# Output projections of a decoder trunk: the last two units run token chunk by token chunk, with three fill buffers, a root on ScalarE and feature-major input and output

## The reference, cut to what matters

```python
def rms_norm(x, gain):
    return x * lax.rsqrt(jnp.mean(x * x, axis=-1, keepdims=True) + 1e-6) * gain
for i in range(4):
    hp, hs = rms_norm(xp, norm_g[i]), rms_norm(xs, norm_g[i])
    # mixer i % 3: q, k, v, g = split(h @ w_in); o = mixer(q, k, v)
    xp = xp + (op * silu(g)) @ w_out      # op: 2048, 1024, 1536, 2048 columns
    xs = xs + ...
```

## Time and profile before

| | |
|---|---|
| median of 3 runs | 3680.8 us (3678.0 to 3686.5) |
| the profiled execution | 3687.3 us |
| its span | 3685.5 us |
| mean granted PE clock | 0.945 |
| PE busy | 3283.7 us, 89% |
| POOL busy | 749.5 us, 20% |

### The profile page before, as it was taken

How to read it: one execution, slowest core, us unless ns; L and a number is a source line. 1 busy time by engine, 2 the same in 40 slices (tenths; PEclk the granted TensorE clock), 3 DMA queues, 4 the chain that set the end, 5 groups by cost and what they waited for, 6 DMA issues and landing times.

```text
span 3685.5 us, 56759 instructions
## 1 busy us (share of the span) xinstructions
PE 3283.7 (89%) x20193; PEld 2945.7 (80%) x20193; DVE 1456.4 (40%) x3286; ACT 1192.5 (32%) x2294; POOL 749.5 (20%) x476
## 2 busy tenths in 40 slices
PE   4999999997996999999968799969799999999788
PEld 3979798886996777777747688859697979798688
DVE  4161514235234334344434566642515161514431
ACT  4232313223123444444432344531323232323211
POOL 3101111113333111110003322233311202011341
PEclk7999999997998999999987899979899999999799
DMA  3647465557212444444443012131124242424611
GB/s 110 226 141 253 141 229 164 198 183 236 90 43 71 128 130 131 130 133 136 136 134 119 18 57 73 56 105 39 39 87 142 86 139 86 129 91 129 226 60 68
DMA packets 512941, 450.90 MB, mean 122 GB/s; under 512 B 24598, under 2 KB 460598, under 8 KB 510674
## 3 DMA queue, kind: packets, MB, share of 16 engines
q1 hardware_dynamic: 406294, 325.75, 29.0%
q10 hardware_dynamic: 106428, 122.27, 9.9%
HBM read 348.56 MB, written 166.50 MB: 140 GB/s over the span
## 4 chain that ended last, share of the span: by engine, by line
PE 70%; DVE 11%; issue 6%; ACT 5%; POOL 4%; DMA 3%; SPq 1%; ACTq 0%; DVEq 0%; POOLq 0%
PE psum L266 17%; PE psum L267 17%; PE psum L268 17%; PE psum L861 3%; POOL Hl L291 3%; PE psum L857 3%; DVE hraw L367 2%; PE psum L1254 2%; ACT Hh L288 2%; PE psum L1227 2%; DMA arena<-scratch_kc 2%; PE psum L853 1%; DVE hraw L328 1%; PE psum L836 1%; PE psum L869 1%
## 5 line engine op out<-in xcount | busy, mean ns | idle before, releaser
L266 PE MATMUL psum<-Hh,Wh 128*128 128x384 f32 (+1 forms) x4896 | 1663.1, 340 | 185.4 <-POOL Hl L291 75.8
L267 PE MATMUL psum<-Hl,Wh 128*128 128x384 f32 (+1 forms) x4896 | 1602.4, 327 | 0.0
L268 PE MATMUL psum<-Hh,Wl 128*128 128x384 f32 (+1 forms) x4896 | 1601.4, 327 | 0.0
L266 PEld LDWEIGHTS psum<-Hh,Wh 128*128 128x128 f32 x4896 | 952.3, 195 | 242.6 <-issue 101.9
L242 POOL TENSOR_TENSOR Wl<-wraw,Wh 128x1024 fp32r<-128x1024 f32 (+1 forms) x208 | 495.2, 2381 | 2388.7 <-ACT Wh L238 2388.7
L267 PEld LDWEIGHTS psum<-Hl,Wh 128*128 128x128 f32 x4896 | 955.2, 195 | 13.9 <-issue 8.2
L268 PEld LDWEIGHTS psum<-Hh,Wl 128*128 128x128 f32 x4896 | 952.1, 194 | 0.0
L238 ACT ACTIVATE Wh<-wraw 128x1024 fp32r<-128x1024 f32 (+1 forms) x208 | 216.1, 1039 | 312.9 <-PE psum L268 224.1
L291 POOL TENSOR_TENSOR Hl<-hraw,Hh 128x384 fp32r<-128x384 f32 (+1 forms) x252 | 226.1, 919 | 327.5 <-ACT Hh L288 327.5
L376 DVE TENSOR_TENSOR xT<-psum,xT 128x384 f32<-128x384 f32 x168 | 86.3, 514 | 370.3 <-PE psum L268 369.8
L288 ACT ACTIVATE Hh<-hraw 128x384 fp32r<-128x384 f32 (+1 forms) x252 | 116.2, 488 | 261.2 <-DVE hraw L367 125.4
(11 more groups left out here) (216 smaller groups left out, 3183.0 us busy)
## 6 DMA issues: line engine op xcount, KB each, us to landing
wraw<-in_ret_w_in SPq DMA_DIRECT2D x96, 512.0 KB, 3.9
scratch_kc<-in_cache_kt SPq DMA_DIRECT2D x64, 512.0 KB, 6.3
scratch_vc<-in_cache_v SPq DMA_DIRECT2D x64, 512.0 KB, 7.0
arena<-in_state_ret ACTq DMA_DIRECT2D x64, 512.0 KB, 6.0
out_ret_state_sample<-arena ACTq DMA_DIRECT2D x64, 512.0 KB, 2.8
arena<-scratch_kc SPq DMA_DIRECT2D x64, 512.0 KB, 5.2
arena<-scratch_vc SPq DMA_DIRECT2D x64, 512.0 KB, 5.4
scratch_on<-arena ACTq DMA_DIRECT2D x80, 256.0 KB, 3.4
```

The lines of the kernel that those rows point to most:

```text
L266: nc.tensor.matmul(out, hi, xh, start=(k == 0), stop=False)
L267: nc.tensor.matmul(out, hi, xl, start=False, stop=False)
L268: last = nc.tensor.matmul(out, lo, xh, start=False, stop=(k == kt - 1))
```

## The change

In every output group that is followed by another fill, units 0 to 5 stay as they were, and units 6 and 7 run by chunk: (6,0), (7,0), (6,1), (7,1), (6,2), (7,2). Chunks are counted by q for banks and semaphores. A tile chunk of H is free after its two last chunks, and its eight new tiles are issued in two halves between the residuals. `hraw` gets a third buffer. The root becomes exp(-0.5 ln(x)) on ACT, with one table set loaded by hand, and DVE's reciprocal goes. x and the gains are laid feature-major outside and loaded straight to `xT`; the squares of the first norm are reduced on PE, eight matmuls a chunk. The result leaves as `y_cols`, straight from `xT`, and is laid out token-major outside. The last group (layer 3) keeps its old order.

```diff
+HR = 3
...
+WAVE_FILLS = (2, 3, 5, 7, 8, 10)
...
+            act.wait_ge(unit_ps, out_ps(unit, wave_last(2) - 1) if wave else ps_val(unit.at(j), 2) - 2 * NC_)
...
+        def out_order(wave):
+
+            if not wave:
+                return [(j, c) for j in range(KT) for c in range(NC_)]
+            return [(j, c) for j in range(KT - 2) for c in range(NC_)] + \
+                   [(j, c) for c in range(NC_) for j in (KT - 2, KT - 1)]
+
+        def out_ps(unit, q):
+            return unit.at(0) * NC_ + (q + 1 + CR_PS)
+
+        def out_ev(unit, q):
+            return unit.at(0) * NC_ + (q + 1 + CR)
+
+        def wave_last(c):
+            return (KT - 2) * NC_ + 2 * c + 1
+
         def unit_bank(j, c):
             return bank[(j + c) % 2]
 
...
                     pe.wait_ge(w_lo, unit.at(j) + 1)
-                pe.wait_ge(unit_ev, ev_val(unit.at(j), c) - 2)
-            out = unit_bank(j, c)[:, 0:w]
+                pe.wait_ge(unit_ev, (ev_val(unit.at(j), c) if q is None else out_ev(unit, q)) - 2)
+            out = (unit_bank(j, c) if q is None else bank[q % 2])[:, 0:w]
             for k in ks:
...
+        def fill_free(act, f, c):
+
+            if f in WAVE_FILLS:
+                act.wait_ge(unit_ps, out_ps(Pos(fill_before(f) - KT), wave_last(c)))
+            elif fill_before(f):
+                act.wait_ge(unit_ps, ps_val(fill_before(f) - 1, c))
...
-        def norm_act(act, layer, c):
+        def norm_root(act, layer, c):
...
-            act.activation(rst[:, 0:w], NB[:, 0:w], ACT.Sqrt, bias=eps_t[:, 0:1], scale=1.0 / D_MODEL)\
-               .then_inc(nrm_sq, 1)
-            fill_parts(act, None, None, f, c)
-
-        def norm_dve(dve, ch, layer, c):
+            if c == 0:
+                act.preload_act_table_set("natural_log_exp_and_others")
+            act.activation(rst[:, 0:w], NB[:, 0:w], ACT.Ln, bias=eps_t[:, 0:1], scale=1.0 / D_MODEL).then_inc(nrm_ln, 1)
+            act.wait_ge(nrm_ln, n + 1)
+            act.activation(rst[:, 0:w], rst[:, 0:w], ACT.Exp, scale=-0.5).then_inc(nrm_sq, 1)
...
+        def norm_dve(dve, ch, layer, c, part=None):
...
-            ch.link(nc.vector.reciprocal(rst[:, 0:w], rst[:, 0:w]))
-            for k in range(KT):
+            for k in half_of(f, part):
                 n = fill_tiles(f, c) + k
...
+                if n >= HR:
+                    dve.wait_ge(h_lo, n - HR + 1)
...
-                    dve.wait_ge(h_lo, n - 1)
+                    dve.wait_ge(h_lo, n - HR + 1)
...
+            dve.wait_ge(unit_ps, out_ps(unit, q))
+            dve.wait_ge(unit_ev, out_ev(unit, q) - 1)
+            nc.vector.tensor_tensor(xT[:, j, c0:c0 + w], bank[q % 2][:, 0:w], xT[:, j, c0:c0 + w], ALU.add)\
+              .then_inc(unit_ev, 1)
...
+            for c in range(NC_):
+                c0, w = CHUNKS[c]
+                for half in range(2):
+                    k0 = 4 * half
+                    src = A["x_cols"][k0 * P:(k0 + 4) * P, c0:c0 + w].rearrange("(k p) t -> p k t", p=P)
+                    sp.dma_start(xT[:, k0:k0 + 4, c0:c0 + w], src).then_inc(xin_ld[2 * c + half], 16)
+                if c == 0:
...
+            for c in range(NC_):
+                c0, w = CHUNKS[c]
+                if c:
+                    pe.wait_ge(nrm_sq, c)
+                for k in range(KT):
+                    pe.wait_ge(sq_done, KT * c + k + 1)
+                    last = nc.tensor.matmul(NB[:, 0:w], ones[:, :], sqb0[:, k, 0:w], start=(k == 0), stop=(k == KT - 1))
+                last.then_inc(nrm_ps, 1)
...
+                    for c0, w, c in [(0, T, NC_ - 1)] if k < KT - 1 else [(*CHUNKS[c], c) for c in range(NC_)]:
+                        sp.wait_ge(unit_ev, ev_val(q_end - KT + k, c))
+                        sp.dma_start(A["y_cols"][k * P:(k + 1) * P, c0:c0 + w], xT[:, k, c0:c0 + w]).then_inc(y_st, 16)
+                sp.wait_ge(y_st, 16 * (KT - 1 + NC_))
...
-                for j in range(KT):
-                    for c in range(NC_):
-                        unit_chunk(pe, unit, j, c, f, FILL_K[f], new_h=(j == 0))
-                        if final and j == KT - 1 and c:
-                            norm_pe(pe, lay + 1, c - 1)
-                if final:
-                    norm_pe(pe, lay + 1, 2)
+                wave = final or x + 1 < len(fills)
+                for q, (j, c) in enumerate(out_order(wave)):
+                    unit_chunk(pe, unit, j, c, f, FILL_K[f], new_h=(j == 0), q=q)
+                    if final and q >= wave_last(0) and (j == KT - 2 or q == wave_last(2)):
+                        norm_pe(pe, lay + 1, c - 1 if j == KT - 2 else c)
...
-                for j in range(KT):
-                    if j < KT - 1:
+                for q, (j, c) in enumerate(out_order(more or final)):
+                    if j < KT - 1 and c == 0:
                         split_hi(act, unit, raw, j + 1, FILL_K[f])
-                    elif x + 1 < len(fills):
-                        split_hi(act, unit, raw, j + 1, FILL_K[fills[x + 1][0]])
-                    elif not last_layer and next_split:
-                        split_hi(act, unit, raw, j + 1)
-                    for c in range(NC_):
-                        if final:
-                            square_act(act, unit, j, j, c, sqb, sqn)
-                            sqn += 1
-                        if j == KT - 1 and x + 1 < len(fills):
-                            fill_parts(act, None, None, fills[x + 1][0], c)
-                        elif final and j == KT - 1 and c:
-                            norm_act(act, lay + 1, c - 1)
+                    if final:
+                        square_act(act, unit, q, j, c, sqb, sqn)
+                        sqn += 1
+                    if (j, c) == (KT - 2, 2) and (more or final and next_split):
+                        split_hi(act, unit, raw, KT, FILL_K[nf], wave=True)
+                    if more and j == KT - 1:
+                        fill_parts(act, None, None, nf, c, 0 if c < 2 else None)
+                    if more and j == KT - 2 and c:
+                        fill_parts(act, None, None, nf, c - 1, 1)
+                    if final and j == KT - 2 and c:
+                        norm_root(act, lay + 1, c - 1)
+                        fill_parts(act, None, None, nf, c - 1, 0)
+                    if final and j == KT - 1 and c:
+                        fill_parts(act, None, None, nf, c - 1, 1)
                 if final:
-                    norm_act(act, lay + 1, 2)
+                    norm_root(act, lay + 1, 2)
+                    fill_parts(act, None, None, nf, 2)
...
-                for j in range(KT):
-                    for c in range(NC_):
-                        residual_dve(dve, unit, j, j, c, final, sqb, sqn)
-                        sqn += final
-                        if j == KT - 1 and x + 1 < len(fills):
-                            stage_dve(dve, st, fills[x + 1][0], c, scale)
-                        elif final and j == KT - 1 and c:
-                            norm_dve(dve, ch, lay + 1, c - 1)
+                for q, (j, c) in enumerate(out_order(more or final)):
+                    residual_dve(dve, unit, q, j, c, final, sqb, sqn)
+                    sqn += final
+                    if more and j == KT - 1:
+                        stage_dve(dve, st, nf, c, scale, 0 if c < 2 else None)
+                    if more and j == KT - 2 and c:
+                        stage_dve(dve, st, nf, c - 1, scale, 1)
+                    if final and j >= KT - 2 and c:
+                        norm_dve(dve, ch, lay + 1, c - 1, j - (KT - 2))
                 if final:
                     norm_dve(dve, ch, lay + 1, 2)
...
-                for j in range(KT):
-                    if j < KT - 1:
-                        split_lo(pool, unit, j + 1, FILL_K[f])
-                    elif x + 1 < len(fills):
-                        split_lo(pool, unit, j + 1, FILL_K[fills[x + 1][0]])
-                    elif not last_layer and next_split:
-                        split_lo(pool, unit, j + 1)
-                    if j == KT - 1:
-                        for c in range(NC_):
-                            if x + 1 < len(fills):
-                                fill_parts(None, None, pool, fills[x + 1][0], c)
-                            elif not last_layer:
-                                fill_parts(None, None, pool, FILL_AT[lay + 1], c)
+                for j in range(KT - 1):
+                    split_lo(pool, unit, j + 1, FILL_K[f])
+                if nf is None:
+                    continue
+                fill_parts(None, None, pool, nf, 0)
+                if more:
+                    fill_parts(None, None, pool, nf, 1, 0)
+                if more or next_split:
+                    split_lo(pool, unit, KT, FILL_K[nf])
+                fill_parts(None, None, pool, nf, 1, 1 if more else None)
+                fill_parts(None, None, pool, nf, 2)
```

216 lines of the change are left out of this document (69 added, 147 removed).

## The result

The changed kernel takes 3562.62 us, median of 4 (3561.82 to 3564.44), against 3682.14 for the kernel before in the same comparison (median of 4, 3678.0 to 3686.5): ratio 0.9676, 95% interval 0.9659 to 0.9693, 119.5 us less. The forecast was 3577.0, or 103.5 less. The profiled execution took 3564.4 us with a span of 3562.6, so its span is 122.9 shorter than that of before.

A forecast was written before the change was run, and what follows sets the result against it. The fill chain over DVE, ACT and POOL was taken as what PE waits for. Gains of 14.6 + 23.4 + 32.5 + 18 + 15 = 103.5 us gave 3577, range 3560 to 3598 (8 in 10: 3555 to 3614).

The forecast's parts named there:

- What bounds: Filling of H: PE waits for the chain DVE writes hraw, ACT copies to Hh, POOL subtracts, with two hraw buffers.
- The tile: In H fills, three buffers with DVE and POOL taking turns: 1.30 us a wide tile against 1.50, 0.94 a narrow one.
- No exclusion: Rival for the fills: DVE and POOL don't exclude each other with three buffers, tiles at 0.98 us; 3527, chance 0.05.
- the slower rival: Rival in every fill: each turn between DVE and POOL costs both sides, tiles at 1.9 us; 3707, chance 0.03.
- First fills: First output fills of layers 0 to 3: shorter by 2.6, 4.0, 5.4 and 2.6 us, sum 14.6.
- Second fills and norms: Second output fills (layers 0, 2, 3) gain 23.4 us; norms with first fills of layers 1, 2, 3 gain 32.5.
- the 1.3 us for a table load that goes: Behind the norm's fill in layers 1 and 2, ACT loads no table: 1.3 us less.
- The signs: Profile signs; wrong if POOL pairs stay at 3.0 us or PE stops over 3 us in each of the last two units.
- Start and end: Start to PE's last wait gains 18 us (bounds 12 and 23); end after the last residual gains 15.
- Third buffer nothing: Rival for the fills: the third buffer brings nothing, tiles stay at 1.50 us; 3616, chance 0.09.
- Only start, end and pace: Rival: PE stays put, its queue holding the reductions ahead of the next unit; only these gains remain; 3610, chance 0.03.
- Order nothing: Rival at group ends: the order by chunk brings nothing, because the fill, not PE, is the chain; 3598, chance 0.05.

## Why the prediction was right, and where it was not

- **What bounds.** Right: the fill's chain between DVE and POOL. Two buffers back cost 41 us, the old order 7.
- **The tile.** 1.30 wide and 0.94 narrow were forecast; 1.28 and 0.89 came (0.91 in the second fill). Taking turns is borne out by instructions that grow while the other engine's runs: DVE's are written as 1.35 and not 0.56, POOL's as 1.32 and not 0.98, and DVE's end 0.42 after POOL's as the earlier trace rows had it. No exclusion (0.98) and the slower rival (over 1.8) are both ruled out by that row.
- **First fills.** 14.6 forecast, 21.7 measured: 5.1, 4.8, 6.7 and 5.1. Two sizes were off. The saving was 0.22 us a wide and 0.24 a narrow tile and came at nearly every interval, where 0.2 at 20 tiles was put in; so a fill became 4.8 to 5.1 shorter and not 4.0. In layer 2 wide tiles come every 1.08 us (1.10 forecast, 1.40 before) and narrow ones every 0.76 (1.07 before), so 6.7 and not 5.4. And the 1.4 us given back in layers 0 and 3 for the third weight's DMA were hardly asked for: PE doesn't stop for that weight in layer 0 and stops 0.55 us in layer 3; the units behind the fill take 85.1 us in layer 0, 85.4 before.
- **Second fills and norms.** 55.9 forecast, 51.6 measured. Of the 4.3 missing, 3.7 are in layer 0's row and 1.3 in layer 1's; layer 3's is 0.7 better. The fills themselves are as forecast: from last Hl to last Hl the second fill of layer 0 gains 10.1 (10.2) and the norm with layer 1's fill 11.5 (11.4). Layer 1's first hraw stands 10.1 us ahead of the last chunk's end, 6.4 forecast; the split (1.86 us for a held hraw), and residuals that let the three buffers run empty, took that back.
- **What fell short behind the norms** is the 1.3 us for a table load that goes, and more. The load goes in layer 1, but there the path moves to SP, which no term of the sum looked at. SP issues 15 small loads for layer 1, one after the other, once the last sum of squares is in. Before, that began 24.9 us ahead of the fill's last Hl, now 13.2, and DVE waits 2.93 us for one of the last of them (the line with `in_c_sel` above). From the last Hl to PE's start on chunk 2 it is 7.2 us, 4.5 before. In layer 2 the load goes too, but ACT then waits 1.33 us for DVE, and nothing is gained.
- **The signs.** PE stopped 5.16 us once between the groups, as said ("some 5 us"), and 10.13 before the last reduction ("near 12"). Inside the last units it stopped 2.11 us in layers 0 and 1. In layer 2, whose second group has chunks half as long, it stopped for longer than the 3 us that the prediction had named as a sign of being wrong, ahead of the reduction between (6,2) and (7,2):

```profile
2531.72 1.65 PE L333 MATMUL psum<-ss,ones 128*128 128x384 f32 x2 [5.63 <-DVE ss L409]
```

By its own sign the order doesn't do there what was said; the row gained the 10.1 us forecast even so.

- **Start and end.** 19.4 for 18, 15.1 for 15.
- **The step that failed** is the one not taken: layer 0's heads were costed at nothing because the change doesn't touch them, though their three second stops were in the trace as "issue". They are 13.2 of the 19.2 us by which the ledger exceeds the forecast (9 to 10 of them the loop's position, the rest of the size of the clock's spread). The other 6.0 are 7.1 too little for the first fills, 4.3 too much for second fills and norms, 1.5 for start and end, and 1.7 of bodies.
- **Luck.** The time lies 2.6 us inside the stated range, and the range was made of the start's bounds and the pace between 1.25 and 1.40, while the loop's position, half of what the ledger has over the forecast, was in neither. Without it the changed kernel would be near 3572 (an estimate: 3562.6 and 9 to 10), close to the forecast, but partly because the errors of the first fills and of the norms have opposite signs.
- **Rivals.** "Third buffer nothing" falls by the run with two buffers. "Only start, end and pace" was priced at 3610; with the old order, which leaves these and the new root, 3571.1 was measured. "Order nothing" (21 us less than forecast) is nearer than it seemed: at its places the order is worth 14 to 15, in the whole time 7 to 12.

## What to carry to other kernels

Where two engines hand tiles to each other through SBUF and the instructions of one are written longer while the other's run, count starts, not durations, and try both halves on one engine: here 0.94 us a tile against 1.28, worth 40 us more. When a removed wait comes back under another engine's name with the same length, the stretch is bound by throughput; shorten the work and leave the order. When a fill ends earlier, look at what its end used to cover, here a list of small loads on SP. And compare the stretches that the change does not touch: here a loop gained or lost 10 us by where it begins in its engine's program, so a new kernel should be tried with a few idle instructions ahead of its loops before its time is put down to the edit. For differences of a few us leave such stretches out of both profiles: two executions of one program then agreed to 0.8 us.

## What the runs showed of the hardware

- PE's second stop after a jump back: 3.37, 2.79 and 1.64 us (nine matmuls into the loop, DMA engines full), 2.15, 2.34 and 2.14 (thirteen matmuls in), each 194 recorded instructions from the program's start, and none where the same code lies elsewhere. In layer 3, the same loop in the kernel before had none.
- Behind one and the same wait the clock needn't do the same: in the changed kernel's third turn PE pauses 1.70 us at the jump in one execution and keeps full clock, 1.88 in the other and has a mean of 0.79 over the next 8 us.
- DVE and POOL in turns: a tile of 384 columns every 1.28 us, with DVE's instruction written as 1.35 (0.56 alone) and POOL's as 1.32 (0.98 alone). With one input on DVE's side 1.08.
- While POOL splits a weight (2.4 us alone), DVE's two-input instruction is written as up to 2.69 us and the split as 2.65.
- An ACT table load took 1.28 us every time.
